# The order inside the chunks of a recurrence, and a state-space product taken for two heads at once

## What is computed

```python
def gdn_chunked(q, k, v, beta, g, S0):          # 4 heads of 128
    A = I + (kb @ k.T) * dec * strict            # one matrix per head and chunk
    sol = triangular_solve(A, [v*beta, kb*exp(G)])
    def step(S, xs):                             # chunks in order
        w = u - wk @ S
        o = (q*exp(G)) @ S + ((q @ k.T) * dec) @ w
        S = exp(gl) * S + kd.T @ w

def ssd_chunked(xdt, g, Bh, Ch, h0):             # 8 heads of 64, 2 groups of B and C
    y_diag = ((Ch @ Bh.T) * dec) @ xdt
    def step(h, xs):
        h = exp(gl) * h + dS                     # h before this is the chunk's h_start
    y = y_diag + (Ch * exp(G)) @ h_start         # "the state's part"
```

## Times and profile before

| | us |
|---|---|
| median of 3 runs (1614.2 to 1616.59) | 1615.87 |
| the profiled execution | 1615.8 |
| its span, first to last instruction | 1614.1 |
| PE busy (87% of the span) | 1401.7 |
| DVE busy (59%) | 959.8 |
| ACT busy (39%) | 632.9 |
| POOL busy (19%) | 308.8 |

### The profile page before, as it was taken

The page is one execution under the profiler, slowest core; times in us unless marked ns, Lnnn a source line. Parts: engine busy times, 40 slices in busy tenths (PEclk is TensorE's granted clock), DMA queues, the critical chain, the costliest instruction groups (busy, mean ns, idle before and its releaser), DMA issues. The chain is left out here.

```text
span 1614.1 us, 22851 instructions
## 1 busy us (share of the span) xinstructions
PE 1401.7 (87%) x8483; PEld 1252.7 (78%) x8483; DVE 959.8 (59%) x1306; ACT 632.9 (39%) x928; POOL 308.8 (19%) x315
## 2 busy tenths in 40 slices
PE   7899999999999569898887945999953999999990
PEld 5899999999999368888887714888842788788870
DVE  4679656322334246777762537445436889999973
ACT  6231121111000345454441013333312788888873
POOL 0011111000000054545510000100001233333320
PEclk9999999999999879999995557999975999999995
DMA  5011122322110334343313055533232599989837
GB/s 197 26 40 45 46 81 90 106 81 81 66 53 28 136 63 97 67 80 83 64 30 134 1 191 163 170 118 100 64 137 102 179 281 274 277 266 275 276 53 263
DMA packets 107767, 197.00 MB, mean 122 GB/s; under 512 B 57852, under 2 KB 78588, under 8 KB 102564
## 3 DMA queue, kind: packets, MB, share of 16 engines
q1 hardware_dynamic: 92116, 138.57, 27.1%
q0 software_dynamic: 15568, 57.37, 12.9%
HBM read 199.99 MB, written 49.41 MB: 155 GB/s over the span
## 5 line engine op out<-in xcount | busy, mean ns | idle before, releaser
L98 PE MATMUL c_ps<-hn_lo,c_whi 128*128 128x368 f32 x936 | 177.8, 332 | 5.6 <-DVEq L182 5.6
L98 PE MATMUL c_ps<-hn_hi,c_wlo 128*128 128x368 f32 x936 | 177.4, 332 | 0.0
L98 PE MATMUL c_ps<-hn_hi,c_whi 128*128 128x368 f32 x936 | 176.6, 331 | 0.0
L98 PEld LDWEIGHTS c_ps<-hn_lo,c_whi 128*128 128x128 f32 x936 | 160.8, 189 | 5.8 <-issue 5.8
L2357 DVE TENSOR_TENSOR e_winlo<-e_win,e_winhi 128x2048 fp32r<-128x2048 f32 x66 | 151.1, 2291 | 20.8 <-ACT e_winhi L2304 19.4
L98 PEld LDWEIGHTS c_ps<-hn_hi,c_wlo 128*128 128x128 f32 x936 | 160.8, 189 | 0.0
L98 PEld LDWEIGHTS c_ps<-hn_hi,c_whi 128*128 128x128 f32 x936 | 159.8, 188 | 0.0
L2304 ACT CAST e_winhi<-e_win 128x2048 fp32r x66 | 122.7, 1913 | 37.5 <-issue 37.5
L82 ACT CAST c_whi<-c_w 128x1024 fp32r<-128x1024 f32 x40 | 42.1, 1052 | 227.4 <-PE c_ps L98 227.4
L2226 POOL DMA_INDIRECT x_rows<-e_ys,idx_out x33 | 81.6, 2472 | 147.1 <-ACT e_ys L2327 147.1
L526 DVE SCALAR_TENSOR_TENSOR c_y<-c_raw,c_taps,c_y 128x1128 f32<-128x1128 f32 x60 | 83.7, 1394 | 6.1 <-DVE c_y L522 0.2
(11 more groups left out here) (471 smaller groups left out, 2837.5 us busy)
## 6 DMA issues: line engine op xcount, KB each, us to landing
e_win<-in_w_gate_up SPq DMA_DIRECT2D x33, 2048.0 KB
e_wdn<-in_w_down SPq DMA_DIRECT2D x33, 1024.0 KB
c_w<-in_w_in SPq DMA_DIRECT2D x40, 512.0 KB, 3.4
rc_eb<-g_rows SPq DMA_DIRECT2D x10, 1040.0 KB, 6.0
o_land<-in_w_out SPq DMA_DIRECT2D x8, 768.0 KB, 5.1
x_rows<-o_land POOLq DMA_DIRECT2D x12, 512.0 KB, 4.0
rc_gb<-g_rows SPq DMA_DIRECT2D x10, 507.0 KB
kv<-in_xT SPq DMA_DIRECT2D x4, 1104.0 KB, 9.5
```

The costliest lines, as they stand in the source:

```text
L98: mm = pe.matmul(dst, left(x, k), right(z, k), start=(n == 0 and k == 0), stop=(n == 2 and k == ks - 1))
```

## The change

- The state's part is taken for two heads at once: four products of the state `SS` (two heads of 64 make 128 rows of the result) with plain C, into a bank of its own (`ys_ps`, in bank Y[0]). The decay exp(G) is put on when DVE takes the result out of PSUM (`yst`, step `sy_state`), from a new tile `egs` that holds the two heads' rows in the two halves of the partitions; a further DVE addition (`sy_sum`) puts `yst` onto x. `cs` goes, and `sy` has eight products in place of sixteen.
- `egs` is loaded by two DMAs of 64 partitions each, behind `eb` in SP's loop; the load waits for DVE's `sy_state` in place of `qg`.
- On DVE `lm` and the `m2t` copies come ahead of `r0`; the copies of `yt` move from ACT to DVE, and `vv` reads `yt` from PSUM in place of SBUF.
- On PE `ks` comes ahead of the `m8` products with r2; `y2`'s first pair waits for `sy_state` too (it writes bank Y[0]).
- On ACT `eb_exp` moves from the end of the chunk before to a place between the `m2` and the `m4` copies of its own chunk, with one exponential more (`egs`) and a smaller first one.
- On POOL `decay(c-1)` comes behind the tables of chunk c.

```diff
             def load_eb(c):
-                wait(v, c - 1, "qg")
+                wait(v, c - 1, "sy_state")
                 if c:
                     sp.wait_ge(decayed, 2 * c)
-                sp.dma_start(eb[:], g_dram[0:R_B, c * CH:(c + 1) * CH].partition_broadcast(P)).then_inc(eb_loaded, 16)
+                cut = slice(c * CH, (c + 1) * CH)
+                sp.dma_start(eb[:], g_dram[0:R_B, cut].partition_broadcast(P)).then_inc(eb_loaded, 16)
+                for half in range(2):
+                    sp.dma_start(egs[half * PB:(half + 1) * PB], g_dram[R_SSD + half:R_Q:2, cut].partition_broadcast(PB)
+                                 ).then_inc(eb_loaded, 16)
...
             for c in range(1, NCH):
-                decay(c - 1)
                 gdn_tables(c)
                 ssd_tables(c)
+                decay(c - 1)
...
             def eb_exp(c):
-                act.wait_ge(eb_loaded, 16 * (c + 1))
-                exp(eb[:, R_SSD:])
-                exp(eb[:, R_G:R_SSD, L - 1:L])
+                act.wait_ge(eb_loaded, 48 * (c + 1))
+                exp(eb[:, R_Q:])
+                exp(eb[:, R_G:R_Q, L - 1:L])
+                exp(egs[:])
...
                 take("m2_", m2, (Y[0], X[1]), c, 1)
+                eb_exp(c)
                 for g in range(2):
                     take("m4_", m4, Y, c, g)
...
                     take("y", y, Z, c, g)
-                    take("yt", yt, X, c, g)
...
-                for g in range(2):
-                    wait(v, c, f"mt{g}")
-                    tt_(r0[:, pair(g), :], mt[:, pair(g), :], over(ident, HP), ALU.add)
+                minus(lm, dec_off, slice(0, HA))
                 take("m2t", m2t, (Z[0], X[0]), 0)
                 take("m2t", m2t, (Z[0], X[0]), 1)
-                minus(lm, dec_off, slice(0, HA))
+                for g in range(2):
+                    tt_(r0[:, pair(g), :], mt[:, pair(g), :], over(ident, HP), ALU.add)
...
-                for g in range(GB):
-                    hs = slice(g * HPG, (g + 1) * HPG)
-                    ins = dve.tensor_tensor(cs[:, hs, :], tokens(bcs[:, GB + g:GB + g + 1], c).to_broadcast([P, HPG, L]),
-                                            eb[:, R_SSD + g * HPG:R_SSD + (g + 1) * HPG, :], ALU.mult)
-                ins.then_inc(v.sem, 1)
...
                 for g in range(2):
-                    wait(a, c, f"yt{g}")
-                    tt_(vv[:, pair(g), :], yt[:, pair(g), :], over(ident, HP), ALU.add)
+                    take("yt", yt, X, g)
+                    tt_(vv[:, pair(g), :], sq_(bank[X[g]]), over(ident, HP), ALU.add)
                 tt_(qg[:], tokens(queries, c), eb[:, R_Q:R_K], ALU.mult)
+                wait(p, c, "sy_state")
+                wait(a, c, "egs")
+                tt_(yst[:], ys_ps, egs[:], ALU.mult)
                 wait(p, c, "sy")
...
                 ins.then_inc(v.sem, 1)
+                wait(v, c, "sy")
+                tt_(tokens(x, c), tokens(x, c), yst[:], ALU.add)
...
-                for g in range(2):
-                    wait(a, c, f"m8_{g}")
+                wait(v, c, "kg")
+                wait(a, c, "m8_1")
+                products(wide(K, HA), kg, S, all_heads).then_inc(p.sem, 1)
+                for g in range(2):
                     wait(v, c, f"r2_{g}")
                     prod(X[g], m8, r2, g)
-                wait(v, c, "kg")
-                products(wide(K, HA), kg, S, all_heads).then_inc(p.sem, 1)
...
-                wait(v, c, "cs")
+                for n in range(4):
+                    mm = pe.matmul(ys_ps[:, n, :], SS[:, 2 * n:2 * n + 2, :].rearrange("p h t -> p (h t)"),
+                                   bcc[:, GB + n // 2, :], start=True, stop=True)
+                mm.then_inc(p.sem, 1)
+                wait(v, c, "cbt")
                 for h in range(HB):
                     half = slice((h % 2) * PB, (h % 2 + 1) * PB)
-                    pe.matmul(sy_ps[half, h // 2, :], xdt[:, h, :], cbt[:, h, :], start=True, stop=False)
-                    mm = pe.matmul(sy_ps[half, h // 2, :], SS[:, h, :], cs[:, h, :], start=False, stop=True)
+                    mm = pe.matmul(sy_ps[half, h // 2, :], xdt[:, h, :], cbt[:, h, :], start=True, stop=True)
...
                 for g in range(2):
-                    wait(a, c, f"yt{g}")
-                    if g == 1:
-                        wait(v, c, "rhs")
+                    wait(a, c, f"y{g}")
+                    wait(v, c, f"yt{g}")
+                    wait(v, c, ("sy_state", "rhs")[g])
```

More of the change, by code:

```diff
@@ L660 @@
 REC_PE = ["kk", "k", "qk", "m2_0", "m2t0", "m2_1", "m2t1", "xt", "m4_0", "m4t0", "r1_0", "m4_1", "m4t1", "r1_1", "btcb",
-          "m8_0", "r2_0", "m8_1", "r2_1", "r3_0", "r3_1", "ks", "y0", "yt0", "y1", "yt1", "sy", "sds",
+          "m8_0", "r2_0", "m8_1", "r2_1", "ks", "r3_0", "r3_1", "y0", "yt0", "y1", "yt1", "sy_state", "sy", "sds",
           "y2_0", "y2t0", "y2_1", "y2t1", "ds_rhs", "y4_0", "z1_0", "y4_1", "z1_1", "z2_0", "z2_1",
           "w0", "w1", "v", "o0", "ds0", "o1", "ds1"]
[L664 to L667, removed]
+REC_DVE = ["m16_0", "mt0", "m16_1", "mt1", "lm", "m2t0", "m2t1", "r0_0", "r0_1", "qkt", "m4t0", "r1_0", "m4t1", "r1_1",
+           "kg", "xdt", "xdd", "r2_0", "r2_1", "r3_0", "r3_1", "cbt", "rhs", "yt0", "vv0", "yt1", "vv1", "qg", "sy_state", "sy", "sy_sum", "z1_0", "z1_1", "ss", "z2_0", "z2_1", "w0", "w1", "s0", "s1"]
+REC_ACT = ["vb", "kd", "m2_0", "m2_1", "eb", "eb_g", "egs", "m4_0", "m4_1", "bt", "m8_0", "m8_1", "y0", "y1", "t_exp", "d_exp",
+           "y2_0", "y2t0", "y2_1", "y2t1", "rhs", "y4_0", "y4_1", "s_exp", "o0", "o1"]
 REC_POOL = ["q", "t", "qm", "tm", "d", "doff", "d16", "s", "sm"]
@@ L690, in recurrence_phase @@
         p, v = Steps(m, "rc_pe", REC_PE, ["v"]), Steps(m, "rc_dve", REC_DVE)
-        a = Steps(m, "rc_act", REC_ACT, ["s_exp", "t_exp", "d_exp", "eb", "eb_g"])
+        a = Steps(m, "rc_act", REC_ACT, ["s_exp", "t_exp", "d_exp"])
         q = Steps(m, "rc_pool", REC_POOL, ["s", "sm", "q", "t", "qm", "tm", "d", "doff", "d16"])
@@ L706, in recurrence_phase @@
         sq, pick, eps = sb("sq", [P, 2, T]), sb("pick", [P, NQK, 36]), sb("eps", [64, 1])
-        spare = sb("spare", [64, 5])
+        spare = sb("spare", [64, 3])
         lnk, lnq = sq[:, 0], sq[:, 1]
@@ L721, in recurrence_phase @@
         bt, xdt, xdd = sb("bt", [L, GB, NB]), sb("xdt", [L, HB, PB]), sb("xdd", [L, HB, PB])
-        cbt, cs = sb("cbt", [L, HB, L]), sb("cs", [P, HB, L])
+        cbt, egs, yst = sb("cbt", [L, HB, L]), sb("egs", [P, 4, L]), sb("yst", [P, 4, L])
         SS, SS1, skip = sb("ss", [P, HB, PB]), sb("ss1", [P, HB, PB]), sb("skip", [P, 4])
@@ L747, in recurrence_phase @@
         sy_ps = KK[:, 0:4 * L].rearrange("p (n t) -> p n t", n=4)
+        ys_ps = bank[Y[0]][:, 0:4 * L].rearrange("p (n t) -> p n t", n=4)
         full, ident, neg_t, neg = masks[:, 0, :], masks[0:L, 0, 0:L], masks[0:L, 1, 0:L], masks[0:L, 2, 0:L]
@@ L918, in _ @@
             gdn_exp(0)
-            eb_exp(0)
             for c in range(NCH):
@@ L952, in _ @@
                     ssd_exp(c + 1)
-                    eb_exp(c + 1)
                 else:
                     copy(spare[:, 2:3], eps[:])
-                    copy(spare[:, 3:4], eps[:])
-                    copy(spare[:, 4:5], eps[:])
                 for g in range(2):
@@ L1153, in _ @@
                     prod(Z[g], m2, m2t, g)
+                    wait(v, c, f"r0_{g}")
                     prod(X[g], m2, r0, g)
```

## The result

The changed kernel took 1598.82 us (median of 4 runs, 1594.91 to 1599.89) against 1615.03 us of before (median of 4) on the same chip: ratio 0.9892, 95% interval 0.9874 to 0.9909. Forecast: 1599.0. The profiled execution took 1599.72 us, its span 1598.1 us.

The account below looks back on a forecast made before the run. PE's list was taken as the path, with 2.65 us idle per chunk to win. Nine chunks at 1.85 us plus 1.2 for the last, less 1.0 for the loop, gave 16.85: 1615.8 to 1599.0 us, range 1592 to 1611.

Parts of the forecast that it names:

- lm, m2t, r0: Start of a chunk: with lm and m2t ahead of r0, PE's next products start 0.93 us earlier.
- ks: PE, ks ahead of r2: y starts 1.1 us earlier in all; the r2 wait becomes two half as long.
- sy and the state's part: PE: four state products 0.89 us plus eight of sy 0.82, 1.71 in place of 1.64; no gain from fusing.
- vv, qg, x: DVE: vv from PSUM saves 2.5 us, x's 0.91 wait goes, 0.5 for yst comes; ds_rhs 1.85 us earlier per chunk.
- The loop: POOL's round, then eb, egs and first gb loads: 23.3 to 24.0 us, just under the chunk's 24.15; 1 us set aside.
- the first rival: POOL-and-loads loop binds at 24.6 to 25.5 us, eight chunks lose 0.5 to 1.4 us: 1602 to 1609; chance 0.15.
- the prediction's own sign: Loop forecast wrong if POOL waits for gb at the head of its round and chunks last over 24.5 us.
- the 9.0: Loads: the first gb must land some 9.0 us after eb's issue, before adding 0.7 to 1.4 us for egs.
- The first chunk: Starts at the lower clock; taken like the others at 1.85 us gain, 1 us either way.
- middle chunks: Recurrence chunks 1 to 8: each gains 1.85 us, less 1/8 us for the loop allowance.
- last chunk: POOL never stopped vv there and x was no wait; only the earlier y2 counts: 1.2 us gain.

Follow-up runs that it names:

- e4: Changed kernel with r0 put back ahead of m2t and lm on DVE: 1607.48 us, ratio 0.9940 to the kernel before.
- e7: e1 with ks put back behind the products with r2 on PE: 1593.88 us, ratio 0.9868 to the kernel before.
- e3: Changed kernel with vv reading yt from SBUF again in place of PSUM: 1645.99 us, ratio 1.0180 to the kernel before.
- e1: Changed kernel with the next chunk's gb loads issued ahead of eb's: 1594.39 us, ratio 0.9859 to the kernel before.
- e2: Changed kernel with egs loaded a second time, into a tile nothing reads: 1603.52 us, ratio 0.9915 to the kernel before.
- e10: e9 with the second half of cs moved on, behind r3: 1593.56 us, ratio 0.9857 to the kernel before.
- e6: Changed kernel without the new state's part (cs and sixteen sy products, no egs or yst): 1630.13 us, ratio 1.0079 to the kernel before.
- e9: e6 with both halves of cs moved between r2 and r3 on DVE: 1598.21 us, ratio 0.9897 to the kernel before.

## Why the prediction was right, and where it was not

- *lm, m2t, r0*: 0.93 us forecast; the xt products follow without a wait, and e4 prices the move at 0.82.
- *ks*: forecast at 0.17 us beyond lm's gain, with waits of 0.25 and 0.25; the waits were 0.15 and 0.10, and e7 shows no gain at all once gb comes early.
- *sy and the state's part*: four products 0.99 and eight 0.86 us (695.90 to 697.75), 1.85 against 1.71 forecast and 1.64 before. No gain from fusing two heads, as said.
- *vv, qg, x*: vv 0.36 an addition (forecast 0.3), POOL's first long operation 1.57 (1.58), qg 0.79 (1.0), y2 14.95 us into the chunk (15.1). The wait of 0.5 us for yst came out near nothing, since the products ahead took longer (in two of the longer chunks it is there, 0.7 us). `ds_rhs` 1.99 us earlier, for 1.85: this is the term that carries the result, and e3 shows that it hangs on vv's operand: with vv in SBUF the change loses 1.8%.
- *The loop*: this step failed. Forecast at 23.3 to 24.0 us, just under the chunk, it came to 13.7 (616.14 to 629.83, POOL's round) and 10.0 to 11.7 from eb's issue to the tables, where 9.0 and 0.7 to 1.4 for the two small loads had been reckoned. It bound, as the first rival had it, in six chunks, and took 0.53 us from a chunk (e1), the lower end of that rival's 0.5 to 1.4, where 1.0 us was set aside for the whole. By the prediction's own sign, POOL waiting for gb and chunks over 24.5 us, it was wrong in four chunks of eight. The two small loads probably cost about what was forecast: two more of them (e2) put the tables 1.2 us further from eb's issue (mean 12.3 for 11.1). It is the 9.0, an estimate for gb without them, that was too low: without egs (e10) gb was there only 10.5 and 10.6 us behind eb's issue in two rounds, in the others by 9.9 to 10.6 at the latest. Why gb's landing varies so from round to round is open. The Trainium skill's page "SBUF — State Buffer", section "Can I just issue two DMAs to hit both halves?", has two transfers to the two halves serialize; by it the prediction had 1.4 us, by eb's rate 0.7, and e2's 1.2 lies between.
- *The first chunk*: taken like the others with 1 us either way, it gained 3.82. Behind its start-up wait PE runs at 1.2 GHz; the clock over one stretch there, before and after:

```profile
590.00:595.00 5.00, 5.00 (x36) 5.00 (x36) 2.67 (x6) 1.29 (x4) 4.92 (x6) 0.60 0.00 0
```

```profile
590.00:595.00 5.00, 4.85 (x44) 4.71 (x43) 3.67 (x7) 1.37 (x4) 4.92 (x6) 0.84 0.00 0
```

After, PE works from 584.89 on without the wait for lm, and full speed comes back at 591.4; before, with that wait of 0.96 us in between, at 593.6. That the missing wait is what brought the clock back earlier is likely, not shown: e4, with the wait, has a first chunk of 36.01 us, e1 and e7 to e10, without it, 32.4 to 34.6.

So 1599.0 came this close by luck: errors cancel. In us: first chunk +1.97; middle chunks 2.06 a chunk in place of 1.85, +1.7; the loop 4.2 in place of 1.0, -3.2; last chunk -0.24. Together +0.2 for the stage. The 1.0 us by which the stage began later is in no term; it makes the profiled execution's gain 16.1 for 16.85. What carried the forecast, PE's idle time and whose operation stands behind POOL's, is what e3, e6, e9 and e10 bear out.

## What to carry to other kernels

Where DVE and POOL work side by side, list the DVE operations that read two SBUF tiles, and place them against POOL's long operations before counting products: here one operand decided between 0.989 and 1.018 (e3), and the place of cs between 1.008 and 0.986 (e6, e10). A change in two halves that together remove the waits can be a loss with one half alone (e6); price a half only in the order in which it will run. And a load issued behind one engine's round and needed at the head of its next makes a loop with the transfers in between: issue that load first.

## What was not expected of the hardware

- The stop between DVE and POOL works both ways. kg (690.56) got in as POOL's third operation began (690.61) and took its usual 0.58 us; POOL's took 1.47 us, 1.06 where DVE did nothing of the kind. The Trainium skill's page "SBUF — State Buffer", section "Who interferes with whom", calls it an exclusive lock that the first to issue holds for the whole instruction, and excepts a DVE operation with one SBUF input; vv's 0.36 us from PSUM and 2.71 us from SBUF agree. A DVE operation that waits is not always the next to go: in e3 the second vv, waiting since 660.38, was passed by decay's first operation (661.82), which took its usual 1.04 us. What decides that is open.
- A wait of 2.4 or 3.2 us on PE costs it again: the granted clock was 0.50 to 0.58 over the 4 us behind it (0.50 is 1.2 GHz), so a wait's price was some 4 to 6.5 us (2.42 and 1.7 in e6; chunks of 28.88 to 30.46 for 23.94 in e3). Waits of up to 1 us showed no such drop: the clock was 1.00 over a whole chunk of before, with waits of 0.97, 0.50 and 0.91 us.
